# An mLSTM block's chunk loop: waits per PSUM bank, the order of VectorE's and TensorE's steps, and where weight splits and gate rows stand

## The reference, cut to what matters

```python
    def step(carry, xs):
        c_mat, n_vec, m = carry
        q_c, k_c, v_c, cum_c, lw_c, lwe_c, qk_c = xs
        log_inter = cum_c + m[..., None]
        m_row = jnp.maximum(log_inter, jnp.max(lw_c, axis=-1))
        s_inter = jnp.exp(log_inter - m_row)
        w_intra = jnp.exp(lw_c - m_row[..., None]) * qk_c
        num = s_inter[..., None] * jnp.einsum('bhck,bhkv->bhcv', q_c, c_mat) \
            + jnp.einsum('bhij,bhjv->bhiv', w_intra, v_c)
        den = s_inter * jnp.einsum('bhck,bhk->bhc', q_c, n_vec) + jnp.sum(w_intra, axis=-1)
        h_c = num / jnp.maximum(jnp.abs(den), jnp.exp(-m_row))[..., None]
        ...
        c_mat = s_keep[..., None, None] * c_mat + jnp.einsum('bhc,bhck,bhcv->bhkv', w_end, k_c, v_c)
        n_vec = s_keep[..., None] * n_vec + jnp.einsum('bhc,bhck->bhk', w_end, k_c)
        return (c_mat, n_vec, m_new), h_c
```

## Time and profile before

| what | value |
|---|---|
| median of 3 runs | 2666.17 us (2665.33 to 2667.7) |
| the profiled execution | 2666.52 us, span 2664.70 us |
| mean granted clock of PE over the span | 0.95 |
| PE busy | 2513.1 us |
| DVE busy | 1387.7 us |
| ACT busy | 842.8 us |
| mLSTM projections with gates, in the trace | about 1102 to 1257 us |
| chunk loop, in the trace | about 1257 to 1391 us |

### The profile page before, as it was taken

The page is one execution under the profiler, slowest core; times in us unless marked ns, Lnnn a source line. Parts: engine busy times, 40 slices in busy tenths (PEclk is TensorE's granted clock), DMA queues, the critical chain, the costliest instruction groups (busy, mean ns, idle before and its releaser), DMA issues.

```text
span 2664.7 us, 38902 instructions
## 1 busy us (share of the span) xinstructions
PE 2513.1 (94%) x15967; PEld 2204.7 (83%) x15967; DVE 1387.7 (52%) x1896; ACT 842.8 (32%) x1211; POOL 265.2 (10%) x203
## 2 busy tenths in 40 slices
PE   6999999999999999989989999998997789899998
PEld 6999999988999999989877888886873446688886
DVE  6677655655444344533555666676127453534433
ACT  4433444444322122312123221223232443322322
POOL 2000222222100000100111000011003101000001
PEclk9999999889999999999779999998998889899999
DMA  3222433335222222222002544452110000122221
GB/s 131 79 83 72 120 91 81 92 65 190 85 95 80 95 94 79 96 79 84 12 1 95 190 159 156 157 189 103 63 64 16 0 0 32 63 95 94 94 95 64
DMA packets 93866, 235.39 MB, mean 88 GB/s; under 512 B 60074, under 2 KB 61700, under 8 KB 69556
## 3 DMA queue, kind: packets, MB, share of 16 engines
q1 hardware_dynamic: 88208, 201.40, 23.3%
q10 hardware_dynamic: 5540, 32.30, 3.5%
HBM read 222.00 MB, written 11.67 MB: 88 GB/s over the span
## 4 chain that ended last, share of the span: by engine, by line
PE 86%; DVE 8%; ACT 3%; issue 2%; DMA 1%; DVEq 0%; ACTq 0%; POOL 0%; POOLq 0%; SPq 0%
PE ps L298 67%; PE ps L1086 1%; PE ps L1076 1%; PE ps L1100 1%; PE ps L302 1%; PE ps L2495 1%; PE ps L2477 1%; PE ps L1872 1%; DVE a_mx L2561 1%; PE ps L1873 1%; PE ps L462 1%; PE ps L1113 1%; PE ps L1112 1%; DVE c_DA L1968 1%; DVE n_y L443 1%
## 5 line engine op out<-in xcount | busy, mean ns | idle before, releaser
L298 PE MATMUL ps<-xa_hi,whi 128*128 128x264 f32 (+1 forms) x2512 | 655.2, 320 | 43.9 <-DVE wlo L321 20.4
L298 PE MATMUL ps<-xa_lo,whi 128*128 128x264 f32 (+1 forms) x2512 | 649.5, 318 | 0.0
L298 PE MATMUL ps<-xa_hi,wlo 128*128 128x264 f32 (+1 forms) x2512 | 648.1, 317 | 0.0
L321 DVE TENSOR_TENSOR wlo<-raw,whi 128x2048 fp32r<-128x2048 f32 x161 | 370.0, 2298 | 255.8 <-ACT whi L314 253.0
L298 PEld LDWEIGHTS ps<-xa_hi,whi 128*128 128x128 f32 x2512 | 417.4, 190 | 88.8 <-DVE wlo L321 22.5
L314 ACT ACTIVATE whi<-raw 128x2048 fp32r<-128x2048 f32 x161 | 307.5, 1910 | 573.5 <-PE ps L298 562.6
L298 PEld LDWEIGHTS ps<-xa_hi,wlo 128*128 128x128 f32 x2512 | 416.4, 190 | 30.1
L298 PEld LDWEIGHTS ps<-xa_lo,whi 128*128 128x128 f32 x2512 | 416.6, 190 | 29.8
L298 PE MATMUL ps<-xb_lo,whi 128*128 128x264 f32 (+1 forms) x1280 | 384.9, 341 | 0.0
L298 PE MATMUL ps<-xb_hi,whi 128*128 128x264 f32 (+1 forms) x1280 | 382.9, 340 | 1.8 <-DVEq L243 1.8
L298 PE MATMUL ps<-xb_hi,wlo 128*128 128x264 f32 (+1 forms) x1280 | 383.1, 340 | 0.0
(11 more groups left out here) (416 smaller groups left out, 2849.4 us busy)
## 6 DMA issues: line engine op xcount, KB each, us to landing
raw<-weights SPq DMA_DIRECT2D x161, 1024.0 KB, 4.9
mod_w<-weights_mod ACTq DMA_DIRECT2D x24, 1024.0 KB, 4.9
g_EC<-scr_g SPq DMA_DIRECT2D x10, 424.0 KB, 5.1
scr_z<-z_st SPq DMA_DIRECT2D x16, 264.0 KB, 4.6
g_D<-scr_g SPq DMA_DIRECT2D x10, 371.0 KB, 5.2
scr_a<-g_AT SPq DMA_DIRECT2D x10, 318.0 KB
h<-x_in ACTq DMA_DIRECT2D x4, 528.0 KB, 8.8
z_b<-scr_z SPq DMA_DIRECT2D x1, 2112.0 KB
```

Source lines behind the costliest of these rows:

```text
L298: mm = pe.matmul(ps[:, at_ + step * c + bank, 0:tn], w[:, hb.slot, k, c * P:(c + 1) * P], x[:, k, t0:t0 + tn], start=(k == 0 and n == 0), ...
L321: dve.tensor_tensor(wlo[:, hb.slot], raw[:, hb.raw_slot], whi[:, hb.slot].bitcast(F32), ALU.subtract).then_inc(S("w_lo"), 1)
```

## The change

PE projects half-blocks 4 and 5 as well before `pe_mls_gates`, and DVE's `dve_mls_gates_tokens` comes after half-block 5's evacuation and the split of that turn instead of after half-block 3's. ACT's exponentials of the gate rows stay at j == 4. In the chunk loop PE's waits on `c_state` and `c_hs`, both ahead of a head so far, are taken apart by bank: the row maxima wait for `c_da` of the previous chunk, the inter scales for `c_state`, the floors for that chunk's maximum (`c_rc`), the scores for `c_hs`; the scores move to the end of the head. The sums of squares move from ahead of the transposes to behind them. DVE writes the state between the maximum and the reciprocal. The splits of `HB_MLS_OUT + 1` move from ahead of the loop into the first chunk: ACT's behind the copies of v, DVE's behind the weighing of k. No arithmetic is changed.

```diff
--- before.py
+++ after.py
@@ -1664,8 +1664,10 @@
             project(0, 1)
             project(1, 0)
             project(1, 1)
+            project(2, 0)
+            project(2, 1)
             pe_mls_gates(pe)
-            with pe.Fori(2, N_MLS_IN // 2) as i:
+            with pe.Fori(3, N_MLS_IN // 2) as i:
                 for s in range(2):
                     project(i, s)
 
@@ -1712,7 +1714,7 @@
                     dve_mls_gates(dve)
                 if j < N_MLS_IN - 1:
                     dve_split(dve, hb.after(2))
-                if j == 3:
+                if j == 5:
                     dve_mls_gates_tokens(dve)
 
         GDN_A, GDN_D, GDN_P = 8, 12, 1
@@ -1829,29 +1831,31 @@
             for i in range(NCH):
                 pe.wait_ge(S("c_st"), i * 4 + 1)
                 for x in range(2):
-                    pe.wait_ge(S("c_state"), i * 2 + x + 1)
-                    pe.wait_ge(S("c_hs"), i * 2 + x + 1)
+                    if i:
+                        pe.wait_ge(S("c_da"), i * 2 + x - 1)
                     for q in range(4):
                         mm = pe.matmul(ps[0:CH, 4 * x, q * CH:(q + 1) * CH],
                                        ident[0:8, 4 * x + q:4 * x + q + 1].to_broadcast([8, CH]), c_rst[0:8, :], start=True, stop=True)
                     mm.then_inc(S("c_nm"), 1)
+                    pe.wait_ge(S("c_state"), i * 2 + x + 1)
                     for m in range(2):
                         mm = pe.matmul(ps[:, 4 * x + 1, m * CH:(m + 1) * CH],
                                        c_pair[32:40, 2 * x + m, :], c_rst[32:40, :], start=True, stop=True)
                     mm.then_inc(S("c_si"), 1)
-                    if x == 0:
-                        pe.wait_ge(S("c_st"), i * 4 + 4)
-                    for q in range(4):
-                        mm = pe.matmul(ps[0:CH, 4 * x + 3, q * CH:(q + 1) * CH], c_kst[:, 2 * x + q // 2, :],
-                                       c_qst[:, 4 * x + q, :], start=True, stop=True)
-                    mm.then_inc(S("c_qk"), 1)
+                    if i:
+                        pe.wait_ge(S("c_rc"), i * 4 + 2 * x - 3)
                     for q in range(4):
                         mm = pe.matmul(ps[:, 4 * x + 2, q * CH:(q + 1) * CH],
                                        ident[64:72, 64 + 4 * x + q:65 + 4 * x + q].to_broadcast([8, P]), c_rst[64:72, :],
                                        start=True, stop=True)
                     mm.then_inc(S("c_fl"), 1)
-                if i:
-                    sums(i - 1)
+                    if x == 0:
+                        pe.wait_ge(S("c_st"), i * 4 + 4)
+                    pe.wait_ge(S("c_hs"), i * 2 + x + 1)
+                    for q in range(4):
+                        mm = pe.matmul(ps[0:CH, 4 * x + 3, q * CH:(q + 1) * CH], c_kst[:, 2 * x + q // 2, :],
+                                       c_qst[:, 4 * x + q, :], start=True, stop=True)
+                    mm.then_inc(S("c_qk"), 1)
                 pe.wait_ge(S("c_vst"), i + 1)
                 for x in range(2):
                     pe.wait_ge(S("c_qs"), i * 2 + x + 1)
@@ -1862,6 +1866,8 @@
                     for q in range(4):
                         mm = pe.transpose(ps[0:CH, 4 * x, q * P:(q + 1) * P], c_vst[:, 4 * x + q, :], ident[:, :])
                     mm.then_inc(S("c_vT"), 1)
+                if i:
+                    sums(i - 1)
                 pe.wait_ge(S("set"), 8 + 8)
                 for x in range(2):
                     pe.wait_ge(S("c_va"), i * 2 + x + 1)
@@ -1915,6 +1921,8 @@
                 for x in range(2):
                     act.wait_ge(S("c_vT"), i * 2 + x + 1)
                     act.activation(c_VA[x][0:CH, :, 0:P], four(4 * x, P, CH), ACT.Copy).then_inc(S("c_va"), 1)
+                if i == 0:
+                    act_split(act, HalfBlock(HB_MLS_OUT + 1))
                 if not last:
                     values(i + 1)
                 for x in range(2):
@@ -1922,14 +1930,12 @@
                     act.activation(c_DA[x][:, :, :], four(4 * x), ACT.Abs).then_inc(S("c_da"), 1)
 
             values(0)
-            act_split(act, HalfBlock(HB_MLS_OUT + 1))
             for i in range(NCH):
                 chunk(i, i == NCH - 1)
             squares(NCH - 1)
             act.activation(misc[0:1, 7:8], ones[0:1, 0:1], ACT.Sqrt)
 
         def dve_mls(dve):
-            dve_split(dve, HalfBlock(HB_MLS_OUT + 1))
             dve.sem_inc(S("c_state"), 2)
             dve.sem_inc(S("c_hs"), 2)
 
@@ -1959,13 +1965,13 @@
                     dve.wait_ge(S("c_kT"), n)
                     dve.tensor_tensor(c_KW[x][0:CH], ps[0:CH, 4 * x + 1, 0:4 * MDK].rearrange("p (a t) -> p a t", a=4),
                                       tok(i, 32, x, MDK), ALU.mult).then_inc(S("c_kw"), 1)
+                if i == 0:
+                    dve_split(dve, HalfBlock(HB_MLS_OUT + 1))
                 for x in range(2):
                     n = i * 2 + x + 1
                     dve.wait_ge(S("c_da"), n)
                     dve.wait_ge(S("c_fl"), n)
                     dve.tensor_tensor(c_DA[x][:, :, :], four(4 * x + 2), c_DA[x][:, :, :], ALU.max).then_inc(S("c_rc"), 1)
-                    dve.wait_ge(S("c_rc"), i * 4 + 2 * x + 1)
-                    dve.reciprocal(c_DA[x][:, :, :], c_DA[x][:, :, :]).then_inc(S("c_rc"), 1)
                     for m in range(2):
                         if i == NCH - 1:
                             break
@@ -1976,6 +1982,8 @@
                                                        ps[:, 4 * x + 1, m * 2 * P:(m + 1) * 2 * P], ALU.mult, ALU.add)
                     if i < NCH - 1:
                         ins.then_inc(S("c_state"), 1)
+                    dve.wait_ge(S("c_rc"), i * 4 + 2 * x + 1)
+                    dve.reciprocal(c_DA[x][:, :, :], c_DA[x][:, :, :]).then_inc(S("c_rc"), 1)
                     dve.wait_ge(S("c_rc"), i * 4 + 2 * x + 2)
                     dve.tensor_tensor(chunk_of(ml[:, 8 + 4 * x:12 + 4 * x], i), four(4 * x + 3), c_DA[x][:, :, :], ALU.mult)\
                         .then_inc(S("c_hs"), 1)
```

## The result

The changed kernel takes 2647.0 us (median of 13 runs, 2635.99 to 2660.99), the kernel before in the same comparison 2664.07 us (13 runs, 2656.56 to 2673.21). The ratio is 0.9935, with an interval of 0.9915 to 0.9955: 17 us faster, between 12 and 23. The forecast was 2652 us, range 2642 to 2661.

What follows compares the result with a forecast made beforehand. PE bounds the kernel, busy 94% of the span, with time to regain in its waits and low clock. Gates 1.2, splits 3.4, waits 4.4 and clock 5 make 14.0; 2666.5 less 14.0 and 0.35 gives 2652 us, range 2642 to 2661.

Steps and rivals of the forecast that it cites:

- gates: Between two mLSTM projections, PE's wait for `c_kd` falls from 5.88 to 4.65 us: gain 1.2 us.
- start: Ahead of the first chunk, PE's 4.41 us wait behind VectorE's split falls to about 1 us: gain 3.4 us.
- the 1.3 us: At four chunk boundaries, PE's wait for the previous chunk's last product goes: 5.2 us, taken as 4.4 after new waits.
- Rival (d): At the boundaries, scores find `c_hs` late and the 1.3 us waits only move: 4.6 us gain, 2662 us; 5%.
- (b): In the chunk loop, idle tipped the clock, which now survives the boundary: 2633 us, or 2645 with one in two; 10%.
- light matmuls and not idleness alone cost the clock: In the chunk loop, 8-row matmuls and scores help lower PE's clock, so it should still fall at every boundary.
- that head's pieces: At a boundary, maxima and inter scales 1.1, scores 0.9, floors 1.1 us, walked in the new order at full clock.
- the clock: In the five chunks, less time at half clock, some 49 us instead of 60.2: gain 5 us, between -3.8 and 10.
- If the transposes still count, low clock lasts about 8 us a boundary: At four boundaries, 8 us of low clock instead of 11.9, gain 7.0 us; about 14 if only products count, loss 3.8.
- Rival (a): At the boundaries, sums hold the clock down, its return counting from the products: 5 to 9 us gain, 2657 to 2661; 25%.
- the sums: In each chunk, sums of squares moved behind v's transposes: by itself neither gain nor cost, the clock decides.
- the state ahead of the reciprocal: At the boundaries, VectorE's state ready at 1335.4 instead of 1338.1, counted within the 4.4 us gain for waits per bank.

Runs made afterwards that it cites:

- e2: Kernel before with only the two splits moved into the first chunk: 2661.41 us, ratio 0.9985 [0.9970, 0.9999].
- e9: Kernel before with row maxima and floors as matmuls of 128 rows, all its waits kept: 2647.40 us, ratio 0.9934.
- e12: The changed kernel again, unaltered, on a third chip: 2648.05 us, ratio 0.9932 to the kernel before.
- e4: Kernel before with only the sums of squares moved behind the transposes: 2675.64 us, ratio 1.0026 [1.0012, 1.0040].
- e5: Changed kernel with the sums of squares back ahead of the transposes: 2655.38 us, ratio 0.9955 to the kernel before.
- e6: Changed kernel with VectorE's reciprocal ahead of the state again: 2639.13 us, ratio 0.9902 to the kernel before.
- e11: Changed kernel with 128-row maxima and floors, `c_kd` formed at j == 4 and the reciprocal ahead of the state again: 2630.56 us, ratio 0.9868 to before.
- e1: Kernel before with only the gates part (two more projections ahead of `pe_mls_gates`, tokens at j == 5): 2665.33 us, ratio 0.9993 [0.9980, 1.0006].
- e3: Kernel before with PE's waits per bank, scores last and state ahead of the reciprocal, sums left in place: 2655.74 us, ratio 0.9961.
- e7: Changed kernel with row maxima and floors as matmuls of 128 rows instead of 8: 2631.21 us, ratio 0.9870 to the kernel before.
- e10: Changed kernel with 128-row maxima and floors and `c_kd` formed at the end of turn j == 4: 2630.67 us, ratio 0.9867 to before.

## Why the prediction was right, and where it was right by luck

**Right by its own steps.** The waits, forecast and (measured): gates 4.65 (4.6), start 1 (0.9), the 1.3 us gone (gone), transposes of k at most 0.8 (0.8). Only the 0.7 us of the scores had no term. Rival (d) falls with that, and (b) too, as five falls are left. Splits covered inside the first chunk: e2 gains 4 us where 3.4 stood, within a wide interval. That light matmuls and not idleness alone cost the clock: e9.

**The step that failed: the length of a head.** The walk took "that head's pieces", 1.1 + 0.9 + 1.1, and laid them end to end in the new order. The pieces overlap once floors follow inter scales: 2.46 us. The trace of before held the sign of it, since the 1.08 us from 1334.33 to 1335.41 carry maxima and inter scales together. Ten heads, 6.8 us that the sum doesn't have. The Trainium skill, "TensorE: Matmul & The Clock Gate", Part 3: Packing small matmuls — row/col tiling, says that matmuls of few rows in different row groups run at the same time. Under "Why this matters for your kernels" the same page of the Trainium skill says that one of 32 rows alone takes as long as one of 128. Both agree with the rows here: 2.46 against 3.26 us for a head, 1.13 against 1.14 for the floors. I weighed that page for its rule on transposes and did not ask its rule on rows of the new order.

**A term mis-sized: the clock.** Forecast 5 us from 49 us of low clock left in the five falls; this execution has 32.6 and e12 41, so that the loop's clock was worth 11 and 8 us. The heads are shorter, so the wide work comes earlier; that this is the reason is argued, as no run changes the heads' length alone. Of the two branches, "If the transposes still count, low clock lasts about 8 us a boundary" was the right one: the four boundaries have 6.6 us each in after and some 8.5 in e12. Taking 10 as a compromise was not needed. "No row here separates transposes from the products behind them" was true of the rows shown, but the trace of before did separate them, in chunk 0 (1274.13, under e4). Rival (a), that return counts from the products, could have been set low from it.

**A term that is no single number: the sums.** "By itself neither gain nor cost; the clock decides" has its first half wrong on both sides. Alone the move costs 7 us, through the clock (e4); in company it hides 12 us of a wait on `c_sq` (e5). In company the gain in time is 5 to 8 us. The walk through the boundary followed the semaphores of heads and transposes, but not the sums' own: with the heads 1.3 us earlier their wait for `c_sq`, 4.8 us in before, would have grown. Had the sums stayed ahead, the 4.4 us for the waits would not have come: e5's loop waits 16.1 + 1.4 = 17.5 us against 5.2 + 4.8 = 10.0 before.

**A term with no value of its own: the state ahead of the reciprocal.** Undone, it costs nothing (e6, e11).

**What the forecast owes to chance.** The loop gave 18 to 21 us where 9.4 stood, and with 4.6 for gates and start the traces would make it 23 to 26; the medians differ by 17. At least 6 us are lost again that no stretch shows for certain: the untouched code behind the loop moves by 3 us either way, and gates and start show as less in time than in waits (e1 1 to 2 us, e5 no better than e3). So the time lies 5 us from the forecast, and within its range, partly because what the sum left out was not kept in full. The parts alone add to -1.9 - 4.0 - 10.4 + 6.9 = -9.4 us, the whole gives -17.3. The 8 us between them are no more than the five intervals leave open, some 9 us together, so this sum alone shows nothing; e4 against e5 shows that the sums' place is worth some 12 us more once the heads no longer wait.

## What to carry to other kernels

When a change reorders short matmuls, look at which rows each one reads: neighbours on different rows may run side by side, and the order decides it. Where PE is busy but the granted clock is low, ask what kind of matmul runs there before taking waits away: here an edit of two lines that gives light matmuls all their rows was worth as much as the whole change on the kernel before, and 16 us more on top of it. And walk every semaphore that the moved work touches through the new order, since waits taken off the heads turned up at the sums (13.9 us in e3 instead of 4.8).

## What the runs showed of the hardware

- PE, busy without a gap, loses its clock in a stretch of 8-row matmuls (after, at 1324.2, with PE busy since 1310): the loop's granted clock is 0.75, and 0.91 with the same waits and columns but 128 rows (e9); 0.82 and 0.96 in the changed kernel (e7). The 128-row matmuls also no longer overlap, and no run separates that from the rows. Whether rows on which the weights are zero count in the same way elsewhere wasn't tried.
- The clock comes back on fp32 transposes alone (before, chunk 0: transposes from 1271.53, clock back at 1274.1 to 1274.3, first product at 1274.13). Sixteen one-column matmuls between transposes and products put off its return in the kernel before from between 1.1 and 3.3 us behind the first product to between 5 and 6 us (e4).
- Matmuls of 8 rows at rows 0, 32 and 64 overlap: 2.46 us for what takes 3.14 in another order and 3.26 with 128 rows.
- The same program varies by 25 us from one execution to the next (2635.99 to 2660.99), and its time follows its mean clock (0.956 to 0.947). Two executions whose traces are kept, 2640.16 and 2650.04 us, have the same waits to 0.1 us. The kernels with 128-row matmuls vary too: 3 us in e7's four runs, but 9 to 12 in the six each of e9, e10 and e11.
